# Attention rows re-ordered: the products with the values after the next row's projection, the scores between two sets of transposes

## The chip, the cores and the metric

One core of one Trainium2 chip runs the whole program. The metric is the device time of one execution in microseconds (us), the median of several runs; the profiler's trace is of one more execution. A line such as L764 is line 764 of the kernel before.

## The reference, cut to what matters

Two transformer blocks over a sequence of 1024 positions of width 1024. The change touches two attentions in them; both go over blocks of 128 queries, and a block sees no later block.

```
forgetting attention, 8 heads of 64:
  q, k = rms_norm per head of the projections
  s = q k^T / 8 + cum_i - cum_j          (causal)
  out = softmax(s) v
differential attention, 8 heads of 2 x 64, values of 128:
  q, k = rope of the projections
  w = softmax(q0 k0^T / 8) - lam * softmax(q1 k1^T / 8)   (masked by blocks of 64)
  out = w v, then rms_norm over the 128 columns, times silu(gate)
```

## The kernel before, in words

Activations and weights of the large products are split into a high and a low part of type fp32r, and each product is three matmuls (`mm3`, L237, its instructions at L239, L240 and L241). Four engines work from four separate programs (tensor, scalar, vector, and the loaders on GpSimd and Sync), each strictly in its own order, and they wait for each other on counted marks: `pe.mark("s0_3")` counts one up on `pe_done`, and another engine waits for that count with `at_mark`. The order of the work is written out by hand in these four programs; there is no planner at run time.

`attend_pe`, `attend_act` and `attend_dve` (L797, L952, L1015) are the three programs of one unit of attention, for both kinds. With `forget` true a unit is a pair of heads of the forgetting attention, so c = 0, 1 counts two heads; with `forget` false a unit is one head of the differential attention and c = 0, 1 counts its two score maps, which are combined on DVE (`weights`, L1035) before they are transposed, so only c = 0 is transposed. There are 4 pairs and 8 heads. All but the last of each run in a hardware loop with `more` true: then the projections q, k, v (and the gate g) of the next pair or head are spread over this unit's rows by a plan (`ATT_PLAN` L754, `DIFF_PLAN` L752), 12 or 24 matmuls of 512 columns to a row. The last unit has no next one; the last pair has instead a `fill`: the layer norm and silu of the convolution branch (`conv_pe`, `conv_act`, `conv_dve`, L1213 to L1274).

A unit has eight rows t = 0 to 7, one to a block of 128 queries; row t has t + 1 blocks of keys. TensorE (PE) does in row t before the change:

1. `projections(t)`: the next unit's part of the plan, into PSUM bank DB. The first part of a half waits until the half before it has been read out of DB (`freed`).
2. `turn(t)`: transposes of the exponentials E0 (and E1, in the forgetting attention) into TBB, which has two banks, TB[0] for key blocks 0 to 3 and TB[1] for 4 to 7. DVE copies them out to PT0 and PT1 (`out_of_banks`, L1056, L1051). Both maps use the same banks: E1's transposes wait for E0's copies.
3. `square_sums` (L794), forgetting attention only, in rows 0, 1, 3 and 5 where a half of q or k is complete: sums of squares for its norm, into DB; ACT must first have squared it (L917), and later takes logarithm and exponential (L923, L925).
4. `scores(t + 1)`: q k^T of both maps into PB (L810, the forget term L818, the mask L822). DVE takes the maxima (`maximum`, L1020), ACT the exponentials with their sums (`exps`, L960), DVE the reciprocals (L1026).
5. `values(t)`: the products with the values (L852) into bank AO; DVE scales them into `ot` (`outputs`, L1064, L1066, L1069).

After row 7 come the last projections, and the transposes of `ot`, which become the next unit of the mixing input. In the differential attention ACT also squares each block of `ot` (`block_out`, L1947), then takes two small functions (L1951, L1954) whose result DVE applies to all of `ot` (L1981) before it is transposed; ACT's silu of the gate (L1005) needs a table of its own, loaded before it and changed back after it (L1006).

An f32 product is issued as two instructions, so `values(t)` has 4(t + 1) of them in a pair and 2(t + 1) in a head.

Of the kernel before, what the change touches and what calls it, by code (L numbers as in the profile page):

```python
# [27 lines left out]
P = 128  # L28
# [3 lines left out]
NB = S // P  # L32
# [47 lines left out]
def build(nc, io, counts, stop=None):  # L80

    made = {"pe": {}, "act": {}, "dve": {}}
    with ExitStack() as ctx:
# [41 lines left out]
        rtok = small_at("rtok", [P, NB], F32)  # L125
# [10 lines left out]
        TB = [TBB[:, 0:HALF], TBB[:, HALF:1024]]  # L136
# [660 lines left out]
        def attend_pe(pe, i, forget, plan, u0, more, fill=None):  # L797


            last_evac = [None]  # L800
# [22 lines left out]
                                start=False, stop=True, skip_group_check=True).then_inc(  # L823
                                    pe_done, pe.mark(f"s{c}_{t}"))

            def turn(t):
                if not more and t:
                    warm(pe, TB[0], 1 if forget else 2)
                for c in range(2 if forget else 1):
                    src = (E0, E1)[c]  # L830
                    if forget:
                        pe.e.wait_ge(act_done, at_mark(pe, "act", f"e{c}_{t}", i))
                    for g in range(1 if t < 4 else 2):
                        if not forget:
                            pe.e.wait_ge(dve_done, at_mark(pe, "dve", f"w{t}_{g}", i))

                        if c:
                            pe.e.wait_ge(dve_done, at_mark(pe, "dve", f"pt0_{t}_{g}", i))
                        elif t:
                            pe.e.wait_ge(dve_done, at_mark(pe, "dve", f"pt{int(forget)}_{t - 1}_{int(t > 4) * g}", i))  # L840
                        transposes(pe, TB[g], lambda b: src[:, b * P:(b + 1) * P],
                                   range(4 * g, min(4 * g + 4, t + 1)), f"T{c}_{t}_{g}")

            def values(t):
                g = 0 if t < 4 else 1
# [27 lines left out]
                        last_evac[0] = f"raw{part[0]}{part[1]}"  # L873


            if i is not None:
                pe.e.wait_ge(act_done, at_last(pe, "act", "cq", i))
                pe.e.wait_ge(dve_done, at_last(pe, "dve", "ck", i))
# [9 lines left out]
                transposes(pe, TB[g], lambda b: vF[:, b * P:(b + 1) * P], range(4 * g, 4 * g + 4), f"vt{g}")  # L888
            for t in range(NB):
                projections(t)  # L890
                if fill:
                    fill(t)
                if t == 0:
                    pe.e.wait_ge(act_done, at_mark(pe, "act", "vt1", i))
                turn(t)
                if forget and more:
                    for x, h in ended(plan, t, "qk"):
                        square_sums(pe, x, h, i)
                        last_evac[0] = f"r{x}{h}"
                if t + 1 < NB:  # L900
                    scores(t + 1)
                values(t)
            projections(NB)
            if not more and not forget:
                warm(pe, TB[0], 3)
# [46 lines left out]
        def attend_act(act, i, forget, plan, more, block_out=None, early=(), fill=None):  # L952
            e = act.e
            busy = [None]

            def exps(t, c):
                n = (t + 1) * P

                e.wait_ge(dve_done, at_mark(act, "dve", f"m{c}_{t}", i))
                e.activation((E0, E1)[c][:, 0:n], PB[c][:, 0:n], ACT.Exp, bias=small[:, c, t:t + 1],  # L960
                             accum_out=small[:, 2 + c, t:t + 1]).then_inc(
                                 act_done, act.mark(f"e{c}_{t}"))

            def halves_out(t):
                for x, h in ended(plan, t, "qkvg"):
                    if x == "g" or not more:
                        continue
                    elif x == "v":
                        value_half_act(act, h, i)
                    elif forget:  # L970

                        if busy[0]:
                            e.wait_ge(dve_done, at_mark(act, "dve", busy[0], i))
                        norm_half_act(act, x, h, i)
                        norm_root_act(act, x, h, i)
                        busy[0] = f"N{x}{h}"
                    else:
                        if busy[0]:
                            e.wait_ge(dve_done, at_mark(act, "dve", busy[0], i))
                        rope_half_act(act, x, h, i)  # L980
                        busy[0] = f"{x}{h}T"

            for t in range(NB):
                if t == 0:
                    for c in range(2):
                        exps(0, c)
                    for g in range(2):
                        e.wait_ge(pe_done, at_mark(act, "pe", f"vt{g}", i))
                        e.activation(vt[:, 4 * g:4 * g + 4, :], TB[g][:, :].rearrange("p (b n) -> p b n", n=P),
                                     ACT.Copy).then_inc(act_done, act.mark(f"vt{g}"))  # L990
                elif block_out:
                    block_out(t - 1)
                halves_out(t)
                if fill:
                    fill(t)
                if t < len(early) and early[t] is not None:
                    if not forget and t == 2:
                        e.wait_ge(pe_done, at_mark(act, "pe", "Dg1", i))
                    high_tile(act, early[t])
                if t + 1 < NB:  # L1000
                    for c in range(2):
                        exps(t + 1, c)
            if not forget:
                e.wait_ge(dve_done, at_mark(act, "dve", "rawg1", i))
                e.activation(sg[:, :], sg[:, :], ACT.Silu).then_inc(act_done, act.mark("silu"))  # L1005
                e.preload_act_table_set(LN_EXP)  # L1006
            if more:

                e.wait_ge(dve_done, at_mark(act, "dve", "Nq1" if forget else "q1T", i))
                e.activation(qT[:, :], qN[:, :], ACT.Copy, scale=0.125).then_inc(act_done, act.mark("cq"))  # L1010
            if block_out:
                block_out(NB - 1)
            halves_out(NB)

        def attend_dve(dve, i, forget, plan, u0, more, early=(), fill=None):  # L1015
# [29 lines left out]
            def out_of_banks(t):  # L1045
                for c in range(2 if forget else 1):
                    for g in range(1 if t < 4 else 2):
                        k = min(4, t + 1 - 4 * g)
                        e.wait_ge(pe_done, at_mark(dve, "pe", f"T{c}_{t}_{g}", i))
                        if not forget:  # L1050
                            e.tensor_tensor(PT0[:, 4 * g:4 * g + k, :],  # L1051
                                            TB[g][:, 0:k * P].rearrange("p (b n) -> p b n", n=P),
                                            rtok[:, 4 * g:4 * g + k].unsqueeze(2).to_broadcast([P, k, P]),
                                            ALU.mult).then_inc(dve_done, dve.mark(f"pt{c}_{t}_{g}"))
                            continue
                        e.tensor_copy((PT0, PT1)[c][:, 4 * g:4 * g + k, :],  # L1056
                                      TB[g][:, 0:k * P].rearrange("p (b n) -> p b n", n=P)).then_inc(
                                          dve_done, dve.mark(f"pt{c}_{t}_{g}"))

            def outputs(t):  # L1060
                e.wait_ge(pe_done, at_mark(dve, "pe", f"pv{t}", i))
# [16 lines left out]
            maximum(0, 1)  # L1078
            weights(0)
            for t in range(NB):  # L1080
                out_of_banks(t)
                if fill:
                    fill(t)
                gates(t)
                if t + 1 < NB:
                    maximum(t + 1, 0)
                    maximum(t + 1, 1)
                outputs(t)
                if t < len(early) and early[t] is not None:
# [1276 lines left out]
```

## Time and profile before

| | |
|---|---|
| median of 3 runs | 2977.0 us (2974.46 to 2977.47) |
| the profiled execution, its own time | 2978.64 us |
| its span in the trace | 2976.6 us |
| PE busy | 2819.4 us, 95% |
| DVE busy | 1609.3 us, 54% |
| ACT busy | 650.7 us, 22% |
| chain that ended last | PE 81%, DVE 12%, ACT 2% of the span |
| forgetting attention, rows of four pairs | about 175 to 496 us |
| differential attention, rows of eight heads | about 2282 to 2855 us |

A busy PE is not a PE at its peak: the end of a matmul is modelled, and two neighbours overlap in the record. A wait is best read as the distance from one start to the next: 512 columns of fp32r follow each other every 0.2275 us, transposes and products with the values every 0.11 to 0.12 us. What is beyond that is a wait. The page's figure for idle time before an instruction is smaller than this by the overlap.

### The profile page before, as it was taken

To read this page: it belongs to the slowest core of one execution; us is meant where nothing else is said; L and a number is where in the kernel's file an instruction comes from. 1 tells how busy PE (TensorE), PEld (TensorE's weight loads), DVE (VectorE), ACT (ScalarE), POOL (GpSimd) and SP (SyncE) were. 2 spreads that over 40 slices of the span, in tenths; PEclk is the share of its full clock that TensorE was granted. 3 is DMA by queue.
4 is the path that set the end of the run, shared out by engine and by line. 5 is a ranking of instruction groups with operands and counts; after the bars stand their busy time and mean duration, and the time that the engine had idled before them with its cause. 6 is when DMAs were issued, how large, how long until landed. Compare 5 with 4: busy or idle time off the path is not lost.

```text
span 2976.6 us, 35289 instructions
## 1 busy us (share of the span) xinstructions
PE 2819.4 (95%) x13352; PEld 2228.9 (75%) x13368; DVE 1609.3 (54%) x2062; ACT 650.7 (22%) x1152; POOL 299.1 (10%) x295
## 2 busy tenths in 40 slices
PE   8889999989999999999999999999998999999996
PEld 6656766768888888877888888888866777777664
DVE  7754445355554554564554454445374666666644
ACT  2133333121111111122111011011042333333321
POOL 0799700000000000001000000000000000000000
PEclk9999999999999999999999999999999999999998
DMA  4211111234443434333222222222242222222121
GB/s 165 88 38 57 56 43 71 99 113 143 140 155 127 165 139 146 141 113 142 85 70 85 85 70 70 92 77 79 77 170 89 71 70 70 71 72 71 50 113 71
DMA packets 48618, 286.61 MB, mean 96 GB/s; under 512 B 6576, under 2 KB 6704, under 8 KB 18608
## 3 DMA queue, kind: packets, MB, share of 16 engines
q1 hardware_dynamic: 21776, 118.50, 11.7%
q0 software_dynamic: 14544, 105.91, 10.4%
q10 hardware_dynamic: 12240, 61.39, 5.4%
q8 instruction: 40, 0.66, 0.1%
q14 instruction: 18, 0.15, 0.0%
HBM read 248.03 MB, written 29.36 MB: 93 GB/s over the span
## 4 chain that ended last, share of the span: by engine, by line
PE 81%; DVE 12%; issue 4%; ACT 2%; DMA 1%; DVEq 0%; SPq 0%; ACTq 0%
PE PB L239 12%; PE PB L241 12%; PE PB L240 12%; PE OBB L239 8%; PE OBB L241 8%; PE OBB L240 8%; PE OBB L852 3%; PE TBB L764 3%; PE PB L810 3%; PE TBB L239 2%; PE TBB L241 2%; PE TBB L240 2%; DVE small L1020 1%; DVE on L1830 1%; DVE cacc L1206 1%
## 5 line engine op out<-in xcount | busy, mean ns | idle before, releaser
L239 PE MATMUL PB<-HH,WH 128*128 128x512 f32 x1520 | 599.8, 395 | 25.6 <-issue 7.7
L241 PE MATMUL PB<-HH,WL 128*128 128x512 f32 x1520 | 594.8, 391 | 0.0
L240 PE MATMUL PB<-HL,WH 128*128 128x512 f32 x1520 | 594.8, 391 | 0.0
L239 PE MATMUL OBB<-HH,WH 128*128 128x512 f32 x992 | 399.6, 403 | 0.1
L241 PE MATMUL OBB<-HH,WL 128*128 128x512 f32 x992 | 387.3, 390 | 0.0
L240 PE MATMUL OBB<-HL,WH 128*128 128x512 f32 x992 | 386.7, 390 | 0.0
L239 PEld LDWEIGHTS PB<-HH,WH 128*128 128x128 f32 x1520 | 287.5, 189 | 93.1 <-issue 28.9
L240 PEld LDWEIGHTS PB<-HL,WH 128*128 128x128 f32 x1520 | 287.6, 189 | 61.9 <-issue 2.2
L241 PEld LDWEIGHTS PB<-HH,WL 128*128 128x128 f32 x1520 | 287.2, 189 | 60.5
L255 DVE TENSOR_TENSOR WL<-RAW,WH 128x2048 fp32r<-128x2048 f32 x101 | 233.1, 2308 | 61.9 <-DMA WH<-units 46.1
L2071 POOL DMA_DIRECT2D WH<-units x85 | 45.5, 535 | 1997.0 <-PE PB L239 1292.4
L241 PEld LDWEIGHTS OBB<-HH,WL 128*128 128x128 f32 x992 | 186.2, 188 | 40.2
L960 ACT ACTIVATE E<-PB,small 128x128 f32<-128x128 f32 (+3 forms) x192 | 140.8, 737 | 345.2 <-DVE small L1020 340.5
L239 PEld LDWEIGHTS OBB<-HH,WH 128*128 128x128 f32 x992 | 186.6, 188 | 35.9 <-DVE WL L255 0.3
L240 PEld LDWEIGHTS OBB<-HL,WH 128*128 128x128 f32 x992 | 186.7, 188 | 35.4
L1020 DVE TENSOR_REDUCE small<-PB 128x1 f32<-128x128 f32 (+3 forms) x192 | 136.2, 751 | 75.7 <-PE PB L822 75.7
L852 PE MATMUL OBB<-vt,PT 128*128 128x64 f32 (+1 forms) x1152 | 150.1, 281 | 11.2 <-DVE PT L1051 11.2
L852 PEld LDWEIGHTS OBB<-vt,PT 128*128 128x128 f32 x1152 | 137.7, 194 | 15.5 <-DVE PT L1051 15.5
L1551 DVE SCALAR_TENSOR_TENSOR G<-PB,par,G 128x1023 f32<-128x1023 f32 (+1 forms) x44 | 56.4, 1282 | 171.2 <-ACT G L1470 168.2
L2104 POOL TENSOR_TENSOR cacc<-cacc,prod 128x496 f32<-128x496 f32 (+29 forms) x90 | 131.2, 1459 | 0.0
L810 PE MATMUL PB<-kT,qT 64*128 64x512 f32 (+3 forms) x576 | 118.9, 517 | 4.9 <-DVE kT L1190 2.3
L764 PE MATMUL TBB<-con,E 128*128 128x128 f32 x576 | 88.5, 279 | 29.9 <-DVE PT L1056 19.6
(319 smaller groups left out, 3752.6 us busy)
## 6 DMA issues: line engine op xcount, KB each, us to landing
RAW<-units SPq DMA_DIRECT2D x85, 1024.0 KB, 4.8
WH<-units POOLq DMA_DIRECT2D x85, 1024.0 KB, 5.1
gs<-units ACTq DMA_DIRECT2D x16, 1024.0 KB, 4.8
gu<-gs ACTq DMA_DIRECT2D x16, 1024.0 KB, 3.9
RAW<-gu SPq DMA_DIRECT2D x16, 1024.0 KB, 4.8
WH<-gu POOLq DMA_DIRECT2D x16, 1024.0 KB, 5.4
tmpd<-xr SPq DMA_DIRECT2D x128, 64.0 KB, 2.0
A<-xT SPq DMA_DIRECT2D x4, 1024.0 KB, 9.8
```

Of the source, the lines that this page charges most:

```text
L239: first = pe.e.matmul(out, wh, xh, start=start, stop=False)
L240: pe.e.matmul(out, wh, xl, start=False, stop=False)
L241: return pe.e.matmul(out, wl, xh, start=False, stop=stop), first
L255: dve.e.tensor_tensor(WL[s][:, :], RAW[:, :], WH[s][:, :].bitcast(F32), ALU.subtract).then_inc(unit_split, 1)
L764: mm = pe.e.transpose(dst[:, c * P:(c + 1) * P], src(b), c_("ident"))
L810: pe.e.matmul(PB[c][:, b:b + w], qT[64 * c:64 * c + 64, t * P:(t + 1) * P], kT[64 * c:64 * c + 64, b:b + w], start=True, stop=False, skip_ ...
L852: mm = pe.e.matmul(AO[:, c * w:(c + 1) * w], (PT0, PT1)[c][:, b, :], vt[:, b, c * w:(c + 1) * w], start=b == 0, stop=b == t, skip_group_ch ...
L960: e.activation((E0, E1)[c][:, 0:n], PB[c][:, 0:n], ACT.Exp, bias=small[:, c, t:t + 1], accum_out=small[:, 2 + c, t:t + 1]).then_inc(act_do ...
L1020: e.tensor_reduce(small[:, c, t:t + 1], PB[c][:, 0:(t + 1) * P], AX, ALU.max, negate=True).then_inc(dve_done, dve.mark(f"m{c}_{t}"))
L1551: e.scalar_tensor_tensor(buf[:, j, d:], PB[b][:, 0:S - d], tap(tile, t, i), buf[:, j, d:], ALU.mult, ALU.add).then_inc(dve_done, dve.mark( ...
L2071: pool.dma_start(WH[n % 2][:, :], source.rearrange("u p n -> p (u n)")).then_inc(hi_full[n % 2], 16)
L2104: pool.tensor_tensor(cacc[:, c, a:b], cacc[:, c, a:b], prod[:, n % 2, 0:b - a], ALU.add).then_inc(conv_taps, 1)
```

## The change

In both attentions `values(t - 1)` follows `projections(t)`, and `values(7)` stands after the rows. In the forgetting attention `turn(t, 0)` (E0) comes before `scores(t + 1)` and `turn(t, 1)` (E1) after them; in rows 0 to 3, where one bank is enough, E1 gets TB[1]. The square sums stay after the first transposes in rows 3 and 5, and follow the scores in rows 0 and 1. DVE and ACT follow: DVE copies E1's transposes between the two maxima, runs the fill after that, and with `more` scales row t - 1 where it scaled row t; ACT puts the norm's root in rows 0 and 1 between the two exponentials, and with `more` squares a block of `ot` at the end of the next row.

```diff
-            def turn(t):
-                if not more and t:
+            def turn_bank(t, c, g):
+                return TB[c if forget and t < 4 else g]
+            def turn(t, c):
+                if not more and t and not c:
                     warm(pe, TB[0], 1 if forget else 2)
...
+                    elif t < 4:
+                        if t:
+                            pe.e.wait_ge(dve_done, at_mark(pe, "dve", f"pt{c}_{t - 1}_0", i))
+                    elif c:
+                        pe.e.wait_ge(dve_done, at_mark(pe, "dve", f"pt0_{t}_{g}", i))
+                    else:
+                        pe.e.wait_ge(dve_done, at_mark(pe, "dve", f"pt1_{t - 1}_{g}" if t > 4 else f"pt{g}_3_0", i))
...
+            def squares(t):
+                if forget and more:
+                    for x, h in ended(plan, t, "qk"):
+                        square_sums(pe, x, h, i)
+                        last_evac[0] = f"r{x}{h}"
...
             for t in range(NB):
                 projections(t)
+                if t:
+                    values(t - 1)
                 if fill:
                     fill(t)
                 if t == 0:
                     pe.e.wait_ge(act_done, at_mark(pe, "act", "vt1", i))
-                turn(t)
-                if forget and more:
-                    for x, h in ended(plan, t, "qk"):
-                        square_sums(pe, x, h, i)
-                        last_evac[0] = f"r{x}{h}"
+                turn(t, 0)
+                if t >= 2:
+                    squares(t)
                 if t + 1 < NB:
                     scores(t + 1)
-                values(t)
+                if t < 2:
+                    squares(t)
+                if forget:
+                    turn(t, 1)
+            values(NB - 1)
             projections(NB)
... (attend_act)
-                elif block_out:
+                elif block_out and not more:
                     block_out(t - 1)
                 halves_out(t)
+                if t >= 2:
+                    root_of(t)
...
                 if t + 1 < NB:
-                    for c in range(2):
-                        exps(t + 1, c)
+                    exps(t + 1, 0)
+                if t < 2:
+                    root_of(t)
+                if t + 1 < NB:
+                    exps(t + 1, 1)
+                if block_out and more and t:
+                    block_out(t - 1)
... (attend_dve)
-                out_of_banks(t)
+                out_of_banks(t, 0)
+                if not forget:
+                    gates(t)
+                if t + 1 < NB:
+                    maximum(t + 1, 0)
+                if forget:
+                    out_of_banks(t, 1)
                 if fill:
                     fill(t)
-                gates(t)
                 if t + 1 < NB:
-                    maximum(t + 1, 0)
                     maximum(t + 1, 1)
-                outputs(t)
+                if not more:
+                    outputs(t)
+                elif t:
+                    outputs(t - 1)
...
             if more:
+                outputs(NB - 1)
```

`root_of` is `norm_root_act` taken out of `halves_out`; `out_of_banks(t, c)` copies map c alone. No DMA and nothing on the queues of Sync and GpSimd is changed.

## Rows read from the trace of the kernel before

**Rows 1.** Waits, 174 to 430 us (three pairs): total us, times, longest.
```profile
PE TBB L764 <- DVE PT L1056: 14.0, 24, 0.9
```
**Rows 2.** Waits, 2284 to 2791 us (seven heads).
```profile
PE OBB L852 <- DVE PT L1051: 10.3, 21, 0.8
PEld TBB L764 <- DVE E L1035: 9.2, 21, 0.7
```
**Rows 3.** Timeline, second pair, row 0: start us, us, instruction [idle before <-releaser].
```profile
267.84 0.27 PE L764 MATMUL TBB<-con,E 128*128 128x128 f32 x1
268.50 0.33 PE L764 MATMUL TBB<-con,E 128*128 128x128 f32 x1 [0.38 <-DVE PT L1056]
269.18 1.12 PE L794 MATMUL OBB<-sqh,con 128*128 128x512 f32 x2 [0.35 <-ACT sqh L917]
270.24 0.70 PE L810 MATMUL PB<-kT,qT 64*128 64x256 f32 x4
270.35 0.69 ACT L923 ACTIVATE rbh<-OBB,epsc 128x512 f32<-128x512 f32 x1 [1.22 <-PE OBB L794]
...
271.63 0.47 PE L239 MATMUL OBB<-HH,WH 128*128 128x512 f32 x1
```
**Rows 4.** Timeline, second pair, rows 6 and 7.
```profile
323.71 1.01 PE L764 MATMUL TBB<-con,E 128*128 128x128 f32 x7 [0.90 <-DVE PT L1056]
...
331.18 0.28 DVE L1066 TENSOR_SCALAR ot<-OBB,small 128x64 f32<-128x64 f32 x1
...
334.89 1.25 PE L764 MATMUL TBB<-con,E 128*128 128x128 f32 x8 [0.35 <-DVE PT L1056]
...
335.59 1.29 DVE L1056 COPY PT<-TBB 128x512 f32<-128x512 f32 x2 [0.15 <-PE TBB L764]
335.99 3.68 PE L852 MATMUL OBB<-vt,PT 128*128 128x64 f32 x32
```
**Rows 5.** Timeline, last pair, rows 5 to 7.
```profile
471.08 1.28 ACT L1248 ACT_TABLE_LOAD   x1
...
477.79 0.99 ACT L960 ACTIVATE E<-PB,small 128x896 f32<-128x896 f32 x1
...
483.07 2.35 DVE L1273 TENSOR_TENSOR cl<-cacc,ch 128x1024 fp32r<-128x1024 f32 x2
...
485.34 2.35 DVE L1020 TENSOR_REDUCE small<-PB 128x1 f32<-128x1024 f32 x2
...
491.64 0.56 PE L852 MATMUL OBB<-vt,PT 128*128 128x64 f32 x4
```
**Rows 6.** Windows, 440 to 444 us: length, busy us of PE, PEld, DVE, ACT, POOL; clock.
```profile
440.00:444.00 4.00, 3.69 (x7) 1.33 (x6) 1.43 (x3) 2.21 (x7) 0.00 (x0) 0.67 0.00 0
```
**Rows 7.** Timeline, second differential head, rows 6 and 7 and its end.
```profile
2411.45 2.34 DVE L1020 TENSOR_REDUCE small<-PB 128x1 f32<-128x1024 f32 x2
2411.59 1.83 PE L852 MATMUL OBB<-vt,PT 128*128 128x128 f32 x14 [0.32 <-DVE PT L1051]
...
2413.72 0.34 DVE L1069 TENSOR_SCALAR ot<-OBB,small 128x128 f32<-128x128 f32 x1
...
2415.53 1.42 DVE L1035 SCALAR_TENSOR_TENSOR E<-E,small,E 128x512 f32<-128x512 f32 x2
2416.41 1.24 PE L764 MATMUL TBB<-con,E 128*128 128x128 f32 x8 [0.24 <-DVE E L1035]
...
2416.83 1.28 ACT L1005 ACT_TABLE_LOAD   x1
2418.45 2.05 PE L852 MATMUL OBB<-vt,PT 128*128 128x128 f32 x16 [0.79 <-DVE PT L1051]
...
2422.21 0.21 ACT L1954 ACTIVATE small<-small 128x8 f32<-128x8 f32 x1
2423.60 1.22 DVE L1981 TENSOR_TENSOR ot<-ot,small 128x1024 f32<-128x1024 f32 x1
...
2425.81 0.82 PE L764 MATMUL TBB<-con,ot 128*128 128x128 f32 x6
```

More of the change, by code:

```diff
@@ L824, in scores @@
                                     pe_done, pe.mark(f"s{c}_{t}"))
-            def turn(t):
-                if not more and t:
+            def turn_bank(t, c, g):
+                return TB[c if forget and t < 4 else g]
+            def turn(t, c):
+                if not more and t and not c:
                     warm(pe, TB[0], 1 if forget else 2)
[L829 to L842, printed above, removed]
+                src = (E0, E1)[c]
+                if forget:
+                    pe.e.wait_ge(act_done, at_mark(pe, "act", f"e{c}_{t}", i))
+                for g in range(1 if t < 4 else 2):
+                    if not forget:
+                        pe.e.wait_ge(dve_done, at_mark(pe, "dve", f"w{t}_{g}", i))
+                        if t:
+                            pe.e.wait_ge(dve_done, at_mark(pe, "dve", f"pt0_{t - 1}_{int(t > 4) * g}", i))
+                    elif t < 4:
[5 more added lines that the diff above has]
+                        pe.e.wait_ge(dve_done, at_mark(pe, "dve", f"pt1_{t - 1}_{g}" if t > 4 else f"pt{g}_3_0", i))
+                    transposes(pe, turn_bank(t, c, g), lambda b: src[:, b * P:(b + 1) * P],
+                               range(4 * g, min(4 * g + 4, t + 1)), f"T{c}_{t}_{g}")
             def values(t):
@@ L890, in attend_pe @@
                 projections(t)
+                if t:
+                    values(t - 1)
                 if fill:
@@ L962, in exps, with root_of @@
                                  act_done, act.mark(f"e{c}_{t}"))
+            def root_of(t):
+                if forget and more:
+                    for x, h in ended(plan, t, "qk"):
+                        norm_root_act(act, x, h, i)
+                        busy[0] = f"N{x}{h}"
             def halves_out(t):
@@ L974, in halves_out @@
                         norm_half_act(act, x, h, i)
-                        norm_root_act(act, x, h, i)
-                        busy[0] = f"N{x}{h}"
                     else:
@@ L1043, in gates, with out_of_banks @@
                         dve_done, dve.mark(f"rawg{h}"))
[L1045 to L1058, printed above, removed]
+            def out_of_banks(t, c):
+                for g in range(1 if t < 4 else 2):
+                    k = min(4, t + 1 - 4 * g)
+                    e.wait_ge(pe_done, at_mark(dve, "pe", f"T{c}_{t}_{g}", i))
+                    if not forget:
+                        e.tensor_tensor(PT0[:, 4 * g:4 * g + k, :],
+                                        TB[g][:, 0:k * P].rearrange("p (b n) -> p b n", n=P),
+                                        rtok[:, 4 * g:4 * g + k].unsqueeze(2).to_broadcast([P, k, P]),
+                                        ALU.mult).then_inc(dve_done, dve.mark(f"pt{c}_{t}_{g}"))
+                        continue
+                    e.tensor_copy((PT0, PT1)[c][:, 4 * g:4 * g + k, :],
+                                  TB[c if t < 4 else g][:, 0:k * P].rearrange("p (b n) -> p b n", n=P)).then_inc(
+                                      dve_done, dve.mark(f"pt{c}_{t}_{g}"))
             def outputs(t):
@@ L1080, in attend_dve @@
             for t in range(NB):
-                out_of_banks(t)
+                out_of_banks(t, 0)
+                if not forget:
+                    gates(t)
+                if t + 1 < NB:
+                    maximum(t + 1, 0)
+                if forget:
+                    out_of_banks(t, 1)
                 if fill:
                     fill(t)
-                gates(t)
                 if t + 1 < NB:
-                    maximum(t + 1, 0)
                     maximum(t + 1, 1)
-                outputs(t)
+                if not more:
+                    outputs(t)
+                elif t:
+                    outputs(t - 1)
                 if t < len(early) and early[t] is not None:
```

## The prediction, made before the change was built

> **What bounds the kernel now.** I read the waits first, each attention by itself. TensorE (PE) sets the end almost everywhere, so only waits on PE's path count. In three pairs of the forgetting attention PE waited for one thing above all, DVE's copy of the first map's transposes, 24 times [rows 1]: eight rows of three pairs. In seven heads of the differential attention it waited 21 times for a copy before the products with the values, and 21 times for the combined exponentials before a transpose [rows 2]: rows 5, 6 and 7 of each head.
>
> Then the timeline. In row 0 of a pair the second map's transpose starts 0.66 us after the first where 0.11 would do, and the square sums come 0.68 after it, for ACT's square [rows 3]: 0.55 and 0.57 lost. Read the same way, the waits between the two maps' transposes in rows 0 to 6 of this pair are 0.55, 0.68, 0.81, 0.95, 0.84, 0.73 and 1.07; row 7 has 0.51. The third pair has 0.62 in its row 6. The page's 14.0 us for all 24 [rows 1] is this less 0.16 us each, by which the record of a transpose (0.27) exceeds its spacing (0.11): 14.0 + 24 x 0.16 = 17.8, against 18.0 by my addition.
>
> **The change part by part.** All sums are against one execution of 2978.6 us (span 2976.6), which is 1.6 above the median of 2977.0; I carry the difference over to the median.
>
> *Rows 2 to 6 of the three looped pairs.* The second map's transposes now come after the scores, which take 1.6 to 2.9 us; the two copies they wait for are done 0.3 to 1.3 us after the first map's transposes. The wait goes: 0.81 + 0.95 + 0.84 + 0.73 + 1.07 = 4.40, twice, and 3.95 in the third, **12.75 us**. What covers the copy is DVE being free: in row 6 it is late, because the norm's last step ran up to the copy, but by my count the copy ends 0.8 us before the scores do. Nothing else becomes late there: the values of the row before need copies and scaled outputs a whole row old, and the square sums of rows 3 and 5 now follow those values and one transpose group, 1.7 us or more after the projection, where ACT's square needs 1.3.
>
> *Rows 0 and 1.* Here the square sums are put behind the scores, and right behind them only one or two transposes stand before the next projection, which needs their bank read by ACT's logarithm. Row 0, put together from [rows 3]: projection ends as before, transpose at 267.84, scores at 268.04 for 0.97 to 269.01, square sums when ACT's square is there, at 269.18 as before, 1.06 us for both; the logarithm runs at 270.35 to 271.03 as before; the next projection starts at 271.08. Before, it started at 271.63 with 0.42 of values done in between, which now come after it. Gain 0.13. Row 1 by the same steps gives -0.02, with the first exponential just ahead of the logarithm on ACT. Together **0.33 us** over three pairs, out of 5.9 us of waits that stood in these two rows.
>
> *Row 7.* No scores follow, so the second map's transposes still wait (0.51, kept). And the values of row 7 wait for the scaled output of row 6, which DVE now makes behind all four copies. The last copy ends at 335.59 + 1.29 = 336.88 [rows 4]; two scalings of 0.28, the second started 0.2 after the first and the first 0.1 before the copy's end, end at 337.27; the values start at 337.33 in place of 335.99. **Lost 1.34 us** a pair, 4.0 in all. Behind this instruction all of PE is queued. The key copy and the low part of the next weights on DVE follow these values as before, at the same distance.
>
> *The last pair.* No projections cover anything here. Each row has one wait less (0.6 to 1.2), but the values now wait for the second copy, which DVE starts only after the first maximum: 0.35 to 0.4 a row; and the fill on DVE comes after the scores, so that the convolution's matmuls in rows 1 and 3 start 0.6 to 0.7 us later. Carried through, the scores of row 5 end about 1.35 earlier than before. From row 5 ACT decides: the second exponential, then 6.7 us from its table load to the next exponential [rows 5]; the scores of row 7 end 1.6 us earlier. Then DVE decides, one thing after the other: maximum 1.2, copies 1.2, the fill's low parts 2.35, second maximum 1.2, ACT's exponential 1.2, reciprocal, copy, two more transposes waiting for copies: 9.0 us from the first maximum to the values of row 7, against 6.3 before (485.34 to 491.64, [rows 5]). Net 9.0 - 6.3 - 1.6 = **1.1 us lost**. All of these are sums of neighbours from the same rows, good to 1 us; I keep -2 to +2.5.
>
> *The clock there.* Around the convolution's matmuls of row 1 PE's granted clock was 0.67 of full in the mean of 4 us [rows 6], so it stood at 1.2 GHz for about 2.6 us of it, after PE had waited twice for under a microsecond shortly before. The new order makes a wait of 1.2 us before row 3's and one of about 2.2 near row 7. By this row another fall may come; the one seen cost 4 x 0.33 = 1.3 us there, and with what lay outside these 4 us I put a fall at 1.7. The sum has none. The Trainium skill (TensorE: Matmul & The Clock Gate, "A second HAM failure mode") describes a clock that falls and rises again where PE idles briefly and often between groups of matmuls. By that rule the last pair would be slower by such a fall; it is a rival below.
>
> *The differential heads.* Moving the values gives nothing in rows 5 to 7, because PE's arrival does not set them. In row 7 DVE begins the maxima at 2411.45 with no idle time before (its ropes and copies ran up to it), then exponential, reciprocal and combination end at 2416.95, and PE's transposes wait for that [rows 7]. The chain starts at DVE, not at PE; the 0.47 us that PE no longer loses before row 6's values are lost before row 7's transposes instead. The same holds from row 5 to row 6. In row 7 the values again wait for the output of row 6, one scaling of 0.34 behind the copies: 2418.71 in place of 2418.45, **0.26 lost** a head, 1.8 over seven. ACT now squares row 6's block before the silu: its chain of two table loads, silu, copy of q, row 7's square and the two small functions, 5.6 us by [rows 7], then starts at 2419.1 and not 2416.83, DVE's scaling of 1.22 ends at about 2425.95, and PE arrives for its transposes at 2425.81 + 0.26 = 2426.07. Hidden, with 0.1 us to spare. The last head keeps its order but for two rows: nothing.
>
> *Switches.* PE changes between kinds of instruction in a new order (mask to projection, projection to values, values to transpose). No row shows most of these; the known ones differ by 0.1 us at most. Taken as nothing; over 24 rows of pairs it leaves +-2.4 us.
>
> **Sum:** -12.75 - 0.33 + 4.0 + 1.1 + 1.8 = -6.2 us, 2970.8 on the median of 2977.0.
>
> **The rivals.**
>
> A. *Another fall of the clock* in the last pair, +1.7: 2972.5. For it: the longer waits before rows 3 and 7, and the row that shows a fall after shorter ones. Against: the wait near row 7 stands close behind the `warm` matmuls, and the fall in row 1 will be there in both orders.
>
> B. *The heads gain after all.* If the waits of [rows 2] went (0.52 + 0.47 + 0.23 + 0.39 = 1.6 a head), 11.3 us more: 2959.5. It needs DVE's chain to begin earlier; nothing in the change starts it earlier, as scores(5) come at the same time.
>
> C. *DVE late in the looped pairs.* The second copy now stands between the maxima and delays everything behind it by 0.4 to 1.3 us; while GpSimd runs its taps the norm's step takes up to 3.2 us. If the transposes after the scores waited 0.7 in rows 4, 5 and 6 of the first two pairs, and the late outputs held the values as much again in one row, 5 us come back: 2976.
>
> D. *The head's end turns into the bound: slower than before.* Place: `ot`'s transposes at the end of each looped head, with ACT's two table loads now behind row 6's square. The sum leaves 0.1 us to spare; every further microsecond of that chain costs seven. Beyond 0.9 us a head the whole gain is gone. If each load, now straight behind a square with accumulation, took a second 1.28 us [rows 7]: 2 x 1.28 x 7 = 17.9 less the spare, 2988. The Trainium skill (ScalarE: Activation LUTs, "What ACT_TABLE_LOAD costs") states a drain of about the load's own length with every switch, which would do just this. Against: in the trace the load begins 0.02 us after the instruction before it and silu 0.01 after the load.
>
> E. *It doesn't do what it says:* in rows 0 and 1 of a pair it moves the waits and removes next to none. That is in the sum; were it so in rows 2 to 6 too, 2977.0 + 6.6 would be left, which no row supports.
>
> **How the numbers follow.** Forecast 0.51 (own range 2967.5 to 2974.5), A 0.25, B 0.08, C 0.09, D 0.07. About 0.2%, 6 us, is what a measurement of this kernel can tell from no change, so the line is at 2971.05, which cuts my forecast in half. Faster: 0.28 of the forecast, 0.06 of A, all of B, with a little of C 0.43. Same: 0.50. Slower: D, 0.07. The range takes in the forecast, A and C, and below it half the last pair's bound and the switches: 2965 to 2976.5. It leaves out B and D.
>
> **What would show it.** After the change: in rows 2 to 6 of a looped pair the transposes of E1 start right behind the mask with no idle time before; in row 7 the values start 0.4 us or more behind the last copy; between the square sums of rows 0 and 1 and the next projection stands a wait for ACT of 0.6 to 0.7. A looped pair is 3.2 us shorter (about 85.6 before), the last pair 1 us longer, a looped head 0.26 longer than 72.9, with its waits moved from before the values to before the transposes in rows 6 and 7. A head shorter by over 0.5 us, a pair's transposes still waiting in rows 2 to 6, or a wait for L1981 before `ot`'s transposes makes me wrong.

## The result, and the profile after

The changed kernel took a median of 2988.75 us in five runs (2985.3 to 2995.8), the kernel before 2977.47 in the five runs beside them: a ratio of 1.0039, with a 95% interval of 1.0027 to 1.0050. The change costs 11.3 us. The forecast was 2970.8, a gain of 6.2, in a range of 2965 to 2976.5.

The profiled execution of after took 2985.7 us, 3.1 less than its median; that of before took 2978.6. The page's engine shares, the chain of work that ended last:

```profile
PE 2829.9 (95%) x13368; PEld 2239.2 (75%) x13368; DVE 1601.2 (54%) x2062; ACT 651.7 (22%) x1152; POOL 300.3 (10%) x295
...
PE 79%; DVE 13%; issue 4%; ACT 3%; DMA 1%; DVEq 0%; SPq 0%; ACTq 0%
```

PE is still the engine that sets the end. What the page does not show is where the time went, so I read periods from the timeline: from the first transpose of the values in one unit (a pair or a head) to the same in the next.

| | looped pairs | last pair and the middle | looped heads (seven) | sum |
|---|---|---|---|---|
| before | 86.0, 85.6, 86.0 | 1849.1 | 6 of 72.9, 73.6 | |
| after | 88.6, 85.8, 86.5 | 1851.4 | 6 of 73.8, 76.1 | |
| after - before | +3.2 | +2.3 | +7.9 | +13.4 |

The two spans differ by only 7.1 (2983.7 against 2976.6), because the first pair began 5.0 us earlier in this execution of after: in the start-up, whose code is the same, the clock was at half for 10.2 us, and for 17.1 in that of before, which by half of the difference accounts for 3.4 of them. The tail was 1.3 shorter; there the clock was at half for 25.3 against 27.6 us. 13.4 - 5.0 - 1.3 = 7.1. I argue from periods and medians, and not from one span.

**The waits are as forecast.** First the waits of PE in the three looped pairs after (what waited, for what; us in total, times, longest):

```profile
PE OBB L859 <- DVE ot L1093: 4.5, 6, 1.2
PE OBB L239 <- ACT rbh L940: 4.2, 6, 0.7
PE TBB L764 <- DVE PT L1083: 1.0, 3, 0.3
```

The wait for the first map's copy, 14.0 us in 24 before [rows 1], is down to 1.0 in 3: only row 7 still has it. In its place stand two others: the values (L859) wait for the scaled output of the row before, twice a pair and at most 1.2 us, and the projection of the next row waits for ACT's logarithm, twice a pair. Row 0 of the second pair, against [rows 3]:

```profile
266.68 1.12 PE L794 MATMUL OBB<-sqh,con 128*128 128x512 f32 x2
267.64 0.27 PE L764 MATMUL TBB<-con,E 128*128 128x128 f32 x1
267.84 0.69 ACT L940 ACTIVATE rbh<-OBB,epsc 128x512 f32<-128x512 f32 x1 [0.16 <-PE OBB L794]
268.58 0.50 PE L239 MATMUL OBB<-HH,WH 128*128 128x512 f32 x1 [0.67 <-ACT rbh L940]
```

Row 7 of the same pair, against [rows 4]:

```profile
327.88 1.25 PE L764 MATMUL TBB<-con,E 128*128 128x128 f32 x8 [0.35 <-DVE PT L1083]
328.57 1.29 DVE L1083 COPY PT<-TBB 128x512 f32<-128x512 f32 x2
329.78 0.27 DVE L1091 TENSOR_SCALAR ot<-OBB,small 128x64 f32<-128x64 f32 x1
329.97 0.27 DVE L1093 TENSOR_SCALAR ot<-OBB,small 128x64 f32<-128x64 f32 x1
330.30 0.88 PE L859 MATMUL OBB<-vt,PT 128*128 128x64 f32 x6 [1.16 <-DVE ot L1093]
```

The copies, the two scalings, and the values 0.06 us behind them, as the prediction put it. Counted from the pair's start, the values of row 7 come at 71.34 us where they came at 74.53: 3.19 earlier, against 4.40 (rows 2 to 6) + 0.11 (rows 0 and 1) - 1.34 = 3.17 in the forecast. Up to here the sum was right, in part by luck: in each pair PE also waited 0.33 us for the scaled output of row 5, before row 6's values (the other three of the six waits for L1093), which the forecast didn't have, and something of the same size that I did not trace was gained elsewhere.

**Then the gain is lost in 12 us.** From these values to the transposes of `ot` in the next unit took 9.05 us before and 12.40 after, with the same instructions: 83.74 in place of 83.58 from the pair's start. In the windows (stretch, its length, busy PE, PEld, DVE, ACT and POOL, granted clock, DMA share, GB/s), after:

```profile
329.00:332.00 3.00, 1.84 (x17) 1.71 (x16) 1.24 (x4) 0.00 (x0) 2.84 (x4) 1.00 0.00 0
332.00:336.00 4.00, 4.00 (x21) 3.90 (x21) 0.45 (x3) 0.00 (x0) 3.92 (x4) 0.56 0.00 0
332.50:336.50 4.00, 4.00 (x18) 3.81 (x17) 0.95 (x3) 0.00 (x0) 3.84 (x5) 0.50 0.00 0
336.00:344.00 8.00, 8.00 (x35) 6.33 (x34) 3.85 (x3) 1.11 (x3) 7.76 (x6) 0.79 0.35 129
```

and before, whose row 7 values start at 335.99:

```profile
332.00:336.00 4.00, 3.65 (x25) 2.89 (x24) 1.70 (x3) 1.54 (x2) 3.84 (x5) 1.00 0.00 0
338.20:342.20 4.00, 4.00 (x26) 3.54 (x25) 2.40 (x4) 0.00 (x0) 3.84 (x4) 1.00 0.00 0
```

After, PE stands still for 1.16 of the 3 us from 329.0, and from 332.5 on its granted clock is at half, 1.2 GHz, for 6.8 us. In the 4 busy microseconds that begin 2.2 us after row 7's values it ran 18 instructions, and before, at the same place (338.2), 26. Before has no such fall in any looped pair; after has one in each of the three, at 243.7 (10.2 us long), 332.5 (6.8) and 417.8 (6.8), 0.8, 2.2 and 1.7 us after the start of the values that ended this wait. A busy PE hides it: the busy share doesn't drop when the clock halves. The waits went as forecast, and this pair as a whole gained nothing.

**In the heads** PE waits in the places that the prediction named, before row 6's and row 7's transposes and before row 7's values (against [rows 2]); waits of PE:

```profile
PE OBB L859 <- DVE ot L1096: 6.7, 6, 1.1
PE TBB L764 <- DVE E L1063: 6.4, 14, 0.5
```

The wait before row 7's values is nearly as long as that of the pairs, in the second head:

```profile
2420.70 2.05 PE L859 MATMUL OBB<-vt,PT 128*128 128x128 f32 x16 [1.13 <-DVE ot L1096]
```

The clock fell behind it in one of the seven heads only (the seventh, 0.2 us after the values' start, for 3.4 us). Yet each head is 0.9 longer where 0.26 was forecast.

### The profile page after: what moved, and what is told of

It is laid out like the page before. It is cut to its first block, busy times and chain, and to the rows that moved or that the text cites. A ratio compares the mean times of both kernels' runs of the same rounds, so it can differ in the third digit from the quotient of the medians.

```text
span 2983.7 us, 35283 instructions
## 1 busy us (share of the span) xinstructions
PE 2829.9 (95%) x13368; PEld 2239.2 (75%) x13368; DVE 1601.2 (54%) x2062; ACT 651.7 (22%) x1152; POOL 300.3 (10%) x295
## 3 DMA queue, kind: packets, MB, share of 16 engines
q1 hardware_dynamic: 21776, 118.50, 11.6%
## 4 chain that ended last, share of the span: by engine, by line
PE 79%; DVE 13%; issue 4%; ACT 3%; DMA 1%; DVEq 0%; SPq 0%; ACTq 0%
PE PB L239 12%; PE PB L241 11%; PE PB L240 11%; PE OBB L239 8%; PE OBB L241 8%; PE OBB L240 8%; PE OBB L859 3%; PE TBB L764 3%; PE PB L810 2%; PE TBB L239 2%; PE TBB L241 2%; PE TBB L240 2%; DVE small L1048 1%; DVE on L1865 1%; DVE cacc L1241 1%
## 5 line engine op out<-in xcount | busy, mean ns | idle before, releaser
L255 DVE TENSOR_TENSOR WL<-RAW,WH 128x2048 fp32r<-128x2048 f32 x101 | 235.0, 2327 | 60.5 <-DMA WH<-units 44.2
L859 PEld LDWEIGHTS OBB<-vt,PT 128*128 128x128 f32 x1152 | 147.2, 200 | 31.0 <-DVE ot L1096 15.6
L859 PE MATMUL OBB<-vt,PT 128*128 128x64 f32 (+1 forms) x1152 | 154.5, 286 | 15.3 <-DVE ot L1096 7.9
L1586 DVE SCALAR_TENSOR_TENSOR V<-PB,par,V 128x1023 f32<-128x1023 f32 (+1 forms) x44 | 56.4, 1282 | 105.6 <-ACT V L1509 102.6
```

The source lines that it names most:

```text
L255: dve.e.tensor_tensor(WL[s][:, :], RAW[:, :], WH[s][:, :].bitcast(F32), ALU.subtract).then_inc(unit_split, 1)
L859: mm = pe.e.matmul(AO[:, c * w:(c + 1) * w], (PT0, PT1)[c][:, b, :], vt[:, b, c * w:(c + 1) * w], start=b == 0, stop=b == t, skip_group_ch ...
L1586: e.scalar_tensor_tensor(buf[:, j, d:], PB[b][:, 0:S - d], tap(tile, t, i), buf[:, j, d:], ALU.mult, ALU.add).then_inc(dve_done, dve.mark( ...
```

## The experiments

Eight kernels, each timed beside the kernel before. That took 2977.7 beside the output ahead, the filled wait, heads as before and pairs as before, and 2978.2 beside the other four. My theory after the result: **the wait of row 7 brings the clock down**, and that is where the pairs' gain went. The rival: the fall comes from the new order as a whole (values behind projections, denser rows before), and the wait is only its neighbour. For the heads there was no theory yet, only +0.9 a head against a forecast of 0.26.

### The output of row 6 ahead of the copies

```diff
             for t in range(NB):
+                if more and t == NB - 1:
+                    outputs(t - 1)
                 out_of_banks(t, 0)
...
-                elif t:
+                elif t and t < NB - 1:
                     outputs(t - 1)
```

> The changed kernel with one thing moved: in row 7 of looped units DVE scales row 6's output before the copies and not behind them. Wait theory (the clock falls at the end of each looped pair because PE waits 1.4 us before row 7's values): that wait goes, the three falls at the pairs' ends go, each pair is 4.5 us shorter than in the kernel before; with the heads at +0.9 and the last pair at +1.4 the time is about 2971. Work theory (it falls because values of row 6, transposes and values of row 7 now stand in one stretch without projections): the falls stay, only the wait of 1.3 us a pair goes, about 2984 to 2985.

Measured: 2972.5, a ratio to before of 0.9978 (0.9969 to 0.9987). The looped pairs took 81.4, 81.1 and 81.9 where before had 86.0, 85.6 and 86.0. Timeline and windows at the same place of the second pair:

```profile
326.55 0.28 DVE L1091 TENSOR_SCALAR ot<-OBB,small 128x64 f32<-128x64 f32 x1 [2.47 <-PE OBB L859]
326.75 0.28 DVE L1093 TENSOR_SCALAR ot<-OBB,small 128x64 f32<-128x64 f32 x1
326.94 1.28 DVE L1083 COPY PT<-TBB 128x512 f32<-128x512 f32 x2
328.37 1.29 DVE L1083 COPY PT<-TBB 128x512 f32<-128x512 f32 x2
...
327.68 1.25 PE L764 MATMUL TBB<-con,E 128*128 128x128 f32 x8 [0.38 <-DVE PT L1083]
328.77 1.45 PE L859 MATMUL OBB<-vt,PT 128*128 128x64 f32 x12
```

```profile
327.00:331.00 4.00, 3.62 (x32) 3.20 (x30) 2.51 (x5) 0.00 (x0) 3.84 (x5) 1.00 0.00 0
331.00:335.00 4.00, 4.00 (x26) 3.54 (x25) 2.42 (x4) 0.00 (x0) 3.84 (x4) 1.00 0.00 0
```

Two instructions of 0.28 us (in heads one of 0.34), moved ahead of the copies, bring 16.2 us. The values start with no wait, the clock stays at full, and values to `ot` take 9.05 us again. The gains over before are 4.60, 4.52 and 4.11 us, where the forecast had, without its term for row 7, 4.51, 4.51 and 4.06. PE still waits 0.3 before row 6's values in each pair, so not every late output is gone. The heads were only 0.31 shorter than after (73.53 against 73.84), which is their own wait in row 7, forecast at 0.26. So 0.6 a head was from something else.

### The wait left in, but filled with matmuls

```diff
+            if forget and more:
+                warm(pe, PB[0], 1)
+                warm(pe, PB[0], 1, 256)
             values(NB - 1)
```

> The changed kernel with three quarters of a warm-up in the wait before row 7's values of the looped pairs: three f32 instructions' worth of 512 and 256 columns, 1.3 us, into a bank nobody reads; the wait stays, but PE works in it. Wait theory: the clock does not fall at the pairs' ends, each pair is about 3.2 us shorter than in the changed kernel, about 2979. Work theory: the falls stay, 2988 or a little more.

This parts waiting from the clock. Its DVE is that of after, and the values can't start earlier. Measured: 2978.5, ratio 1.000 (0.9991 to 1.0009), 10.2 under after. Timeline of PE at row 7 of the second pair, and windows:

```profile
330.24 1.46 PE L304 MATMUL PB<-con 128*128 128x512 f32 x4
331.56 1.10 PE L859 MATMUL OBB<-vt,PT 128*128 128x64 f32 x8
```

```profile
329.00:332.00 3.00, 2.85 (x16) 1.92 (x16) 2.36 (x6) 0.00 (x0) 2.92 (x4) 1.00 0.00 0
332.00:336.00 4.00, 4.00 (x34) 3.87 (x34) 0.52 (x3) 0.00 (x0) 3.84 (x5) 1.00 0.00 0
```

The values come 71.31 us after the pair's start, in after 71.34, so the wait lasts as long. But PE was busy 2.85 of the 3 us, and in none of the three pairs did the clock fall at the end: values to `ot` in 9.15 us. What differs between these two kernels from there on is the clock alone: the pairs are 84.5, 82.5 and 83.3 long, against 88.6, 85.8 and 86.5. (The pair of 84.5 also holds a fall of 3.4 us in its row 0, far from this place.)

### The late output alone, in the kernel before

```diff
-                outputs(t)
+                if not (more and forget) or t < NB - 2:
+                    outputs(t)
+                elif t == NB - 1:
+                    outputs(t - 1)
+                    outputs(t)
```

> The kernel before with one thing added: in looped pairs DVE scales row 6's output in row 7, behind the four copies, so that PE waits 1.3 us for it before row 7's values. Nothing else of the change is in it. Wait theory: the clock falls at the end of the three looped pairs here too; each pair 1.3 us for the wait and 3 to 4 for the fall longer, 12 to 15 us in all, 2990 to 2993. If it takes the longer stretch of small products as well (the wait alone is not enough): only +4, 2982.

The whole order of before stays, but for two scalings in DVE's queue. Measured: 2996.5, ratio 1.0059 (1.0045 to 1.0073), 18.3 us over before and more than expected.

```profile
345.84 0.28 DVE L1064 TENSOR_SCALAR ot<-OBB,small 128x64 f32<-128x64 f32 x1
346.03 0.28 DVE L1066 TENSOR_SCALAR ot<-OBB,small 128x64 f32<-128x64 f32 x1
346.36 1.47 PE L852 MATMUL OBB<-vt,PT 128*128 128x64 f32 x9 [1.17 <-DVE ot L1066]
```

```profile
343.00:346.00 3.00, 1.84 (x14) 1.19 (x12) 2.65 (x5) 1.30 (x2) 2.84 (x4) 1.00 0.00 0
346.00:350.00 4.00, 3.64 (x21) 3.64 (x21) 0.31 (x2) 0.00 (x0) 3.85 (x4) 0.65 0.00 0
350.00:356.00 6.00, 6.00 (x21) 5.29 (x21) 3.13 (x4) 0.00 (x0) 5.83 (x5) 0.50 0.00 0
```

The values start 1.36 later than in before (1.29 and 1.27 in the other two pairs), the term the prediction put at 1.34, and the clock falls in all three pairs, for 10.2, 10.2 and 6.8 us. The rival falls: no new order is needed. The pairs took 92.2, 91.9 and 90.6, so 6.2, 6.3 and 4.6 more than before. From the values to the transposes of `ot`, where the wait is over, a fall of 10.2 us costs 4.9 of path, and one of 6.8 costs 3.3. After gives the same prices: values to `ot` are 4.9 longer in its first pair, whose fall lasted 10.2, and 3.3 in the two others. The loss here is larger than I expected because two of three falls were long.

These falls are read from one profiled execution of each kernel. The granted clock of every timed execution says the same: its mean is 0.983 in after and in the kernel with the heads as before (next section), 0.982 here, and 0.986 to 0.988 in before and in the six others. For after against before that is 0.0046 of 2988 us, twice over as the clock falls to half: some 27 us at half clock, where its three falls make 24.

### Heads in their old order, and pairs in theirs

Changed kernel with the differential heads as before (PE, ACT and DVE queues):

```diff
-                if t:
+                if forget and t:
                     values(t - 1)
...
                 if forget:
                     turn(t, 1)
-            values(NB - 1)
+                else:
+                    values(t)
+            if forget:
+                values(NB - 1)
```

(its queues of DVE and ACT are put back in the same way)

> The changed kernel with the order of the differential heads put back to that of before; the forgetting pairs as changed. By the gaps of the two traces the heads hold +0.9 us each, 6.3 over seven, and what clock falls they bring: expected 6 to 8 us less than the changed kernel, 2981 to 2983, still slower than before by the pairs' clock falls (+4 to +6). If the heads cost nothing and the whole loss were the clock in the pairs: 2988.

Measured: 2981.3, ratio 1.0010 (1.0001 to 1.0019), +3.6. The heads are 72.9 to 73.0 again, and in the pairs the falls stand at the same place as in after: 6.8, 10.2 and 6.8 us.

The other half: the kernel before, with the heads changed and the pairs not:

```diff
                 projections(t)
+                if t and not forget:
+                    values(t - 1)
...
-                values(t)
+                if forget:
+                    values(t)
+            if not forget:
+                values(NB - 1)
```

> The other half: forgetting pairs in the order of before, differential heads as changed. Heads +0.9 each: +6.3, 2983.8, a head's period 73.8 against 72.9, and no fall of the clock near the pairs' ends. If heads and pairs were independent, this one and the one with the heads as before add up to the changed kernel's +11.3.

Measured: 2984.8, ratio 1.0025 (1.0016 to 1.0033), +7.1. The heads are 73.8 to 73.9 (the seventh 74.5) and no pair has a fall. 3.6 + 7.1 = 10.7 of the 11.3: the two halves hardly act on each other, and the heads are the larger one.

### The pairs alone, with the output ahead; and without the last pair

The next kernel is the first experiment's for the pairs, and before's order for the heads.

> The part of the change that pays, alone: pairs as changed with row 6's output scaled ahead of the copies, heads in the order of before. By the gaps measured: three pairs of about 81.5 against 85.9 (-13.2), last pair +1.4, heads 0: about -12, 2966. If the heads' loss of the earlier run were not in their order but came with the pairs' state, it would stay near 2972.

Measured: 2967.5, ratio 0.9960 (0.9947 to 0.9974): 10.7 under before. Looped pairs of 81.5, 81.2 and 81.9: 13.1 less than before over the three.

Then the same, with the last pair (`not more`) in before's order too:

```diff
-                if forget and t:
+                if forget and more and t:
                     values(t - 1)
...
                 turn(t, 0)
+                if forget and not more:
+                    turn(t, 1)
```

> As the pairs alone, with the last pair (the one with the convolution's norm in it) in the order of before too. By the trace of the changed kernel that gives back 1.4 us (values of row 7 start 58.6 and not 60.0 us after the pair's begin): about 2964.5. If the last pair's loss was the clock and not the chain, the same within the noise as the run with the pairs alone.

Measured: 2964.7, ratio 0.9955 (0.9942 to 0.9969). The period of the last pair and the middle is 1848.07 in place of 1850.87, and the medians differ by as much, though their intervals overlap. A single period is less sure than that looks, since it holds 1770 us of other work, with falls of the clock that come and go. The pair itself tells more. From its start to row 7's values it takes 58.6 us in before and 59.96 in after, and 56.90 in this kernel and 58.27 in the one with the pairs alone: 1.37 more in the new order both times. From these values to the transposes of `ot` it is 4.25 in all ten profiled kernels. So the last pair's new order costs 1.37 us. The other 1.7, by which before and after are both longer than these two, is the fall of 3.4 us in row 1 [rows 6]. It stands in four of the ten profiled executions (before, after, output ahead, heads as before), in either order, so it doesn't hang on the change.

### Rows 0 and 1 of the heads

In after the third head loses 0.17 us by row 1's transposes (13.43 from its start, 13.26 before) and 0.45 by row 2's (20.95, 20.50). From there on it is level until row 7. What DVE and PE do around row 1 of after's second head:

```profile
2363.37 0.68 DVE L1070 TENSOR_TENSOR sg<-OBB,rbx 128x512 f32<-128x512 f32 x1
2363.69 0.28 PE L822 MATMUL PB<-maskb,identb 128*128 128x128 bf16 x2
2364.11 0.50 PE L239 MATMUL OBB<-HH,WH 128*128 128x512 f32 x1
```

The gate multiply (L1070) reads the bank `DB` that the next projection writes. Before, the values of the row stood between mask and projection and covered it. Now the projection comes right behind the mask and waits until 2364.05; the whole trace of the heads has this wait 14 times, two a head:

```profile
PEld OBB L239 <- DVE sg L1070: 3.7, 14, 0.3
```

The kernel that tests it is the first experiment's, with the values of rows 0 and 1 back in their own rows, in heads only:

```diff
-                if t:
+                if t and (forget or not more or t >= 3):
                     values(t - 1)
...
                 if forget:
                     turn(t, 1)
+                elif more and t < 2:
+                    values(t)
```

> The kernel with row 6's output ahead of the copies, and in the heads rows 0 and 1 with their products in their own rows as before, the others as changed. If the heads lose 0.46 us because these products no longer cover DVE's gate multiply, which must read the bank before the next projection, a looped head goes from 73.5 to 73.05. If the loss is in the order of PE's instructions itself (switches), it stays within 0.1 of 73.5.

Measured: 2964.6, ratio 0.9955 (0.9940 to 0.9971). Heads of 73.07, against 73.53 with those rows moved: 0.46 of the missing 0.6 a head, and 3.2 us over seven. The last 0.1 a head against before (72.95) stays open. The head's row 1 and 2 transposes are at 13.25 and 20.49 from its start, as before. Row 7 of this kernel's second head shows why the change doesn't help a head (values of row 6, DVE's combination, row 7's transposes):

```profile
2398.57 1.82 PE L859 MATMUL OBB<-vt,PT 128*128 128x128 f32 x14
2399.91 1.42 DVE L1065 SCALAR_TENSOR_TENSOR E<-E,small,E 128x512 f32<-128x512 f32 x2
2400.79 1.24 PE L764 MATMUL TBB<-con,E 128*128 128x128 f32 x8 [0.40 <-DVE E L1065]
```

The values end at 2400.39, and PE waits 0.40 for the combination, which itself waits for nothing that PE does late. In the third head the projections of row 6 started 1.9 us earlier than before (48.10 against 50.01) and its transposes at 53.15 against 53.10. PE's head start is lost in full.

## Why the prediction was wrong

Point by point, in its own terms.

- **Rows 2 to 6 of the looped pairs, -12.75: right.** The values of row 7 came 3.19 earlier with row 7's wait in; with it out, the three pairs are 13.1 to 13.2 us shorter. That it fits to 0.1 is luck: a wait of 0.3 a pair before row 6's values was not in the sum, and was made up for elsewhere.
- **Rows 0 and 1, -0.33: right in mechanism**, with ACT's logarithm waited for 0.7 us in each. Its own size is below what the periods can part.
- **Row 7 of the pairs, "Lost 1.34 us a pair, 4.0 in all": the step that failed.** The wait was 1.27 to 1.36 in the kernel that has nothing else. But I priced it as time in which PE does nothing, and it also halved the clock behind it. The prediction weighed the clock, under "The clock there", for the last pair alone, with the words "The sum has none". For the looped pairs it has no word on the clock, although the change makes there the pair's longest wait (1.16 in the second pair, where before had 0.90 at most), right behind a shorter one. Rival A had the mechanism at the wrong place: one fall of 1.7 us for the last pair, where there were three in the looped pairs, of 4.9, 3.3 and 3.3 us, 11.6 in all. The last pair had the wait that A feared, and no fall behind it in any of the six profiled kernels with its new order. Timeline and window, after:

```profile
490.19 1.16 PE L764 MATMUL TBB<-con,E 128*128 128x128 f32 x8 [1.96 <-DVE PT L1083]
```

```profile
489.00:492.00 3.00, 1.81 (x16) 1.73 (x17) 2.50 (x5) 0.25 (x2) 0.00 (x0) 1.00 0.00 0
```

- The Trainium skill (TensorE: Matmul & The Clock Gate, "A second HAM failure mode: psum-queue depth-cycling") describes a clock that falls with brief idle stretches repeated between groups of matmuls. The traces agree for the looped pairs: falls with the waits of 0.35 and 1.16 us, none where the last one is gone or filled. I asked it only for the last pair. It would not have told these kernels apart: the looped pairs of before wait briefly in every row too, up to 0.9 us, and their clock does not fall.
- **The last pair, +1.1: right to 0.3**, 1.37 measured. The +2.3 in the table of periods holds this and chance in the 1770 us behind it.
- **The heads, +0.26 each: right as a term, 0.31 measured, but not the whole: the second step that failed.** I looked at rows 5 to 7 and at the end, and counted rows 0 to 2 at nothing. There the values had covered the gate multiply, and taking them away costs 0.46. About 0.1 more was not traced. In all a head lost 0.86 to 0.93, 6.3 us over seven, against 1.8. The seventh head of the profiled execution also had a fall of 3.4 us near 2790 (76.1, against 74.5 in the kernel with only the heads changed); it stands in that execution's table and not in this sum.
- **Rival B, heads gain: false**, for the reason given. **Rival C, DVE late: false** for the transposes, which do not wait in rows 2 to 6; of its late outputs 0.33 us a pair came true, 1.0 in all. **Switches as nothing: not refuted**, since the pairs' sum came out, but nothing tested them alone. **Rival D, the head's end: false.** Its 2988 is next to the measured 2988.75 by accident. At the end of the second head after:

```profile
2420.89 0.19 ACT L1982 ACTIVATION_READ_ACCUMULATOR sqd<-ot 128x1 f32 x1
2421.10 1.28 ACT L1033 ACT_TABLE_LOAD   x1
2422.39 1.06 ACT L1033 ACTIVATE sg<-sg 128x1024 f32<-128x1024 f32 x1
...
2426.48 0.21 ACT L1989 ACTIVATE small<-small 128x8 f32<-128x8 f32 x1
2426.72 1.23 DVE L2016 TENSOR_TENSOR ot<-ot,small 128x1024 f32<-128x1024 f32 x1 [0.79 <-ACT small L1989]
2428.05 1.05 PE L764 MATMUL TBB<-con,ot 128*128 128x128 f32 x8
```

DVE's scaling ends at 2427.95 and PE's transposes begin 0.10 us later, with no idle time. The Trainium skill (ScalarE: Activation LUTs, "What ACT_TABLE_LOAD costs") has a drain with each switch; by it D would have come true. These rows show none: the load begins 0.02 us after the accumulator's read, takes 1.28, and silu begins 0.01 after it.

So the slower side held 0.07 of the chance, all of it on D. The sum with what the runs gave: -12.75 - 0.33 + 4.0 + 1.4 + 6.3 + 11.6 for the falls = +10.2, against the measured 11.3, whose interval is some 3 us to either side. The first pair of after also reached row 7 some 0.8 us later than this sum has it. There PE waited 0.9 us for the low part of a weight tile (L255) that DVE makes. The same wait stands in the two other profiled kernels whose first pair began at 171 to 172 us, pairs in before's order among them, and is 0.3 us at most in those that began at 175 or later: it goes with the early start and not with the change.

## What to carry to other kernels

Price a new wait of PE twice: its length, and what may follow at half clock; here 1.36 us cost up to 6.3. Its length alone does not decide it: nearly the same length in the heads rarely brought the clock down, and a longer one in the last pair never did. So remove such a wait, or fill it with matmuls, and measure. When late work is put into an in-order queue, put the short instruction whose result releases another engine ahead of the long ones: 0.56 us of scalings ahead of 2.6 us of copies made the same change a gain. And when work is moved off a place, list what it covered there, the read-out of every bank included, before asking what it will cover next.

Two versions are the best, level within the noise. One has the looped pairs' new order with the output ahead, and all else as before: 2964.7 against 2978.2, ratio 0.9955 (0.9942 to 0.9969). The other is the last experiment's, 2964.6.

## What the runs showed of the hardware

- A wait of 1.17 us in TensorE, behind one of 0.35 and beside short f32 products, was followed by 6.8 or 10.2 us at 1.2 GHz in all nine looped pairs that had it (after, heads as before, late output). At this place there was no fall in the fifteen pairs of the five kernels in which it was removed or filled, nor in the six of before and of the heads-only kernel. In before's order this one added wait was enough, and two f32 products of 512 and 256 columns (1.46 us in the record) in it were enough to prevent the fall.
- The length of a wait does not decide it alone. A wait of 1.12 us behind one of 0.40, before row 7's values of the heads, was followed by a fall (3.4 us) in 2 of the 21 looped heads that had it (after, pairs as before, filled wait), and in none of the 49 heads without it. A wait of 1.96 us in row 7 of the last pair was followed by none in six of six executions.
- A fall of 3.4 us cost 1.7 us of path (last pair), one of 6.8 cost 3.3 to 3.4, and one of 10.2 cost 4.9 to 5.0, the two longer ones in nine looped pairs of three kernels: half its length or a little less.
- What stays open: why the falls last 6.8 us in some pairs and 10.2 in others; why the looped pairs' wait always brings one and that of the heads seldom; whether the short wait ahead of it is needed, since no kernel takes it away alone.
